# First layer's values and gate as seven block products instead of eight

## Chip, cores and metric

One core of a Trainium2 chip runs one program. The metric is the device time of one execution in microseconds, the median of three runs. Engine names in profile rows: PE is TensorE (PEld its weight loads), DVE is VectorE, ACT is ScalarE, POOL is GpSimd, SP is the queue that only issues transfers. Everything is computed in float32 by pairs: each operand of a matmul is split into a rounded part (`hi`) and a remainder (`lo`), and a product is the sum of three matmuls, hi by hi, hi by lo and lo by hi.

## The reference

The input is 512 tokens of width 1024, followed by a retention layer, a latent-attention layer and a third block with pooling, neighbourhood attention and an MLP. The change lies in the first layer, the part before its output projection:

```python
hproj = x @ w_in                       # 1024 -> 4*256 (q), 4*256 (k), 4*512 (v), 4*512 (gate)
q = rope(q); k = rope(k) * 256 ** -0.5
o[n] = sum over m <= n of gamma_h ** (n - m) * (q[n] . k[m]) * v[m]     # per head, 4 heads
o = (o - mean(o)) * rsqrt(var(o) + 1e-5)                                # per head and token, over 512
return (o * silu(gate)) @ w_out
```

## The kernel before

**Tiles.** `x` lies transposed in SBUF as `xhi` and `xlo`, eight tiles of 128 features by 512 tokens. The weights of one head come in six panels of 1 MB (128 by 2048): query, key, values (two panels of 512 features each), gate (two panels of 256 columns each). `split_dots` (L565 to L569) issues the three matmuls of a product; nearly all of them have 512 columns. PSUM has eight banks; A is the first four and B the last four.

**Panels.** For each panel SP loads it into one of two `stage` buffers (`load`, L576) once GpSimd is done with the panel before last. ScalarE rounds it to `whi` in two halves (`split_hi`, L1451), GpSimd subtracts to get `wlo`, also in two halves (`split_lo`, L718, L724). TensorE waits for each half.

**One head on TensorE** (`rest`, L984, and the loop at L1036): query and key, 48 matmuls each, into B; values for all four token tiles into A, 96; the scores, 24 narrower ones, into B; the first half of the gate, 48; the 30 matmuls of scores by values into B (L1002); the second half of the gate, 48; 16 transposes of the normed output (L1015). The gate is computed transposed, with its features on the partitions.

**VectorE** (loop at L2392) rotates query and key (L2399 to L2402 read PSUM, L2404 and L2405 read SBUF alone), makes the low parts of query, key, values and scores (`lo_of`, L2082), applies the decay, takes the statistics of the head's output (L2433 to L2443), norms it (L2447), and multiplies its transpose by the gate into `oT` (L2452). **ScalarE** (`head`, L1629) rounds what VectorE then subtracts from, and takes tanh and square root.

**Behind the heads** comes the output projection (`AO`), which is already computed as seven block products in 14 steps of 24 matmuls (`seven`, L953). It wants sums of weight blocks, made in DRAM while the heads run: ScalarE's queue issues copies (`copy_blocks`, L1506, four 1 MB copies at a time; `copy_b11`, `copy_b22` for a later stage) and GpSimd's queue issues transfers that add onto them (`sum_step`, L734; `up_sum`, L746). The steps of AO need an operand split (`operand_hi`, `operand_lo`, `combine`) and a panel split (`weights_hi`, `weights_lo`); VectorE makes most of those remainders, GpSimd those of the first two steps.

## Time and profile before

| | |
|---|---|
| median of 3 runs | 1414.61 us (1414.3 to 1414.74) |
| the profiled execution | 1414.12 us, of which the profile's span is 1412.3 us |
| TensorE | busy 1393.4 us, 99% of the span, granted clock 0.997 |
| VectorE, ScalarE, GpSimd | 65%, 49%, 27% of the span |
| DMA | 260 MB, mean 184 GB/s |
| heads 1 to 3 | 77.8 us each; head 0 ends at 84.5 us, head 3 at 319.65 us |

A busy share says how much of the time an engine had work. An engine's row in the timeline gives its start and its length; matmuls overlap, so what one costs is the distance between two starts, and not its length. The number in brackets behind a row is the time that the engine stood idle ahead of it, and what ended that.

### The profile page before, as it was taken

To read this page: it belongs to the slowest core of one execution; us is meant where nothing else is said; L and a number is where in the kernel's file an instruction comes from. 1 tells how busy PE (TensorE), PEld (TensorE's weight loads), DVE (VectorE), ACT (ScalarE), POOL (GpSimd) and SP (SyncE) were. 2 spreads that over 40 slices of the span, in tenths; PEclk is the share of its full clock that TensorE was granted. 3 is DMA by queue.
4 is the path that set the end of the run, shared out by engine and by line. 5 is a ranking of instruction groups with operands and counts; after the bars stand their busy time and mean duration, and the time that the engine had idled before them with its cause. 6 is when DMAs were issued, how large, how long until landed. Compare 5 with 4: busy or idle time off the path is not lost.

```text
span 1412.3 us, 19358 instructions
## 1 busy us (share of the span) xinstructions
PE 1393.4 (99%) x7412; PEld 1203.4 (85%) x7412; DVE 919.2 (65%) x1562; ACT 698.8 (49%) x1131; POOL 388.2 (27%) x192
## 2 busy tenths in 40 slices
PE   9999999999999999999999999999999899999998
PEld 7888888888889888888888888778888899998887
DVE  6444354549961865545544479946877878789896
ACT  4323232236554533443443356648956465666554
POOL 5334254541034343343334230035314100000000
PEclk9999999999999999999999999999999999999999
DMA  7257946946533988975796557353122576446552
GB/s 292 90 194 204 296 155 164 263 115 258 188 103 129 289 235 221 312 176 157 210 302 161 162 207 284 135 193 126 64 83 75 165 184 173 128 173 213 197 187 111
DMA packets 53890, 260.26 MB, mean 184 GB/s; under 512 B 5568, under 2 KB 10304, under 8 KB 28224
## 3 DMA queue, kind: packets, MB, share of 16 engines
q1 hardware_dynamic: 37152, 163.04, 33.3%
q0 software_dynamic: 5760, 41.95, 14.9%
q10 hardware_dynamic: 10912, 54.40, 11.3%
q8 instruction: 41, 0.67, 0.2%
q14 instruction: 25, 0.20, 0.0%
HBM read 252.03 MB, written 91.23 MB: 243 GB/s over the span
## 4 chain that ended last, share of the span: by engine, by line
PE 89%; DVE 7%; ACT 2%; POOL 1%; issue 1%; DMA 0%; SPq 0%; DVEq 0%; ACTq 0%; POOLq 0%
PE bank L567 23%; PE bank L569 23%; PE bank L568 23%; PE bank L1176 6%; PE bank L1238 4%; PE bank L1127 3%; PE bank L1155 1%; DVE wlo L2082 1%; DVE wlo_a L2082 1%; DVE xlo L2082 1%; DVE br_lo L2082 1%; PE bank L1318 0%; PE bank L913 0%; PE bank L1015 0%; DMA stage<-in_w 0%
## 5 line engine op out<-in xcount | busy, mean ns | idle before, releaser
L724 POOL TENSOR_TENSOR wlo<-stage,whi 128x1024 fp32r<-128x1024 f32 (+2 forms) x116 | 291.9, 2543 | 544.8 <-ACT whi L1458 544.8
L1458 ACT ACTIVATE whi<-stage 128x1024 fp32r<-128x1024 f32 (+2 forms) x120 | 122.2, 1069 | 87.3 <-PE bank L569 64.3
L567 PE MATMUL bank<-xhi,whi 128*128 128x512 f32 (+1 forms) x428 | 149.3, 349 | 3.2 <-DVE xlo L2082 1.8
L569 PE MATMUL bank<-xhi,wlo 128*128 128x512 f32 (+1 forms) x428 | 148.5, 347 | 0.0
L568 PE MATMUL bank<-xlo,whi 128*128 128x512 f32 (+1 forms) x428 | 148.3, 346 | 0.0
L1461 ACT ACTIVATE whi<-stage 128x1024 fp32r<-128x1024 f32 (+2 forms) x125 | 118.0, 989 | 40.3 <-PE bank L569 29.4
L2082 DVE TENSOR_TENSOR wlo<-stage,whi 128x1024 fp32r<-128x1024 f32 x108 | 123.4, 1168 | 14.7 <-ACT whi L1461 14.7
L567 PEld LDWEIGHTS bank<-xhi,whi 128*128 128x128 f32 x428 | 81.1, 189 | 13.5 <-issue 2.2
L567 PE MATMUL bank<-whi,xhi 128*128 128x512 f32 (+1 forms) x236 | 91.4, 387 | 1.1 <-POOL wlo L724 1.1
L569 PE MATMUL bank<-whi,xlo 128*128 128x512 f32 (+1 forms) x236 | 90.4, 383 | 0.0
L568 PE MATMUL bank<-wlo,xhi 128*128 128x512 f32 (+1 forms) x236 | 90.3, 383 | 0.0
L569 PEld LDWEIGHTS bank<-xhi,wlo 128*128 128x128 f32 x428 | 81.0, 189 | 10.3
L568 PEld LDWEIGHTS bank<-xlo,whi 128*128 128x128 f32 x428 | 81.1, 189 | 9.8
L2082 DVE TENSOR_TENSOR wlo_a<-stage,whi_a 128x1024 fp32r<-128x1024 f32 (+1 forms) x60 | 71.4, 1217 | 18.5 <-ACT whi_a L1461 18.5
L1461 ACT ACTIVATE whi_a<-stage 128x1024 fp32r<-128x1024 f32 (+1 forms) x56 | 53.8, 1008 | 22.8 <-PE bank L569 19.9
L567 PEld LDWEIGHTS bank<-whi,xhi 128*128 128x128 f32 x236 | 44.8, 190 | 10.4 <-POOL wlo L724 1.3
L569 PEld LDWEIGHTS bank<-whi,xlo 128*128 128x128 f32 x236 | 44.7, 190 | 8.4
L568 PEld LDWEIGHTS bank<-wlo,xhi 128*128 128x128 f32 x236 | 44.9, 190 | 8.0
L1176 PE MATMUL bank<-xhi,whi 128*128 128x512 f32 x128 | 50.7, 396 | 0.0
L1176 PE MATMUL bank<-xhi,wlo 128*128 128x512 f32 x128 | 50.0, 391 | 0.0
L1176 PE MATMUL bank<-xlo,whi 128*128 128x512 f32 x128 | 49.9, 390 | 0.0
L2082 DVE TENSOR_TENSOR pt_lo<-bank,pt_hi 128x384 fp32r<-128x384 f32 (+1 forms) x48 | 26.6, 595 | 34.9 <-ACT pt_hi L1461 34.9
(451 smaller groups left out, 3943.5 us busy)
## 6 DMA issues: line engine op xcount, KB each, us to landing
stage<-in_w SPq DMA_DIRECT2D x79, 1024.0 KB, 4.9
tsum<-in_w ACTq DMA_DIRECT2D x32, 1024.0 KB, 14.5
stage<-tsum SPq DMA_DIRECT2D x32, 1024.0 KB, 4.8
tsum<-in_w POOLq DMA_DIRECT2D x16, 1024.0 KB, 10.1
tsum<-tsum POOLq DMA_DIRECT2D x16, 1024.0 KB, 10.1
stage<-in_w SPq DMA_DIRECT2D x8, 1152.0 KB, 6.3
usum<-in_w POOLq DMA_DIRECT2D x8, 1024.0 KB, 9.9
stage<-usum SPq DMA_DIRECT2D x32, 256.0 KB, 3.8
```

Of the source, the lines that this page charges most:

```text
L567: pe.matmul(dst, a_hi, b_hi, start=start, stop=False)
L568: pe.matmul(dst, a_hi, b_lo, start=False, stop=False)
L569: return pe.matmul(dst, a_lo, b_hi, start=False, stop=stop)
L724: pool.tensor_tensor(lo[:, r], stage[p % 2][:, r], hi[:, r].bitcast(F32), ALU.subtract).then_inc(w_lo, 1)
L1127: last = pe.matmul(bank[4 + q][:, 0:w], left, right, start=i == 0, stop=i == 4)
L1155: last = pe.transpose(dst[min(kt, 2)][:, at:at + P], prob[:, src:src + P], ident[:, :])
L1176: last = pe.matmul(bank[0][:, :], left[:, k, f], right[:, k, :], start=i == 0, stop=i == 23)
L1238: last = pe.matmul(bank[m][:, :], left[:, k, m * P:(m + 1) * P], right[:, k, :], start=i == 0, stop=i == 23)
L1458: act.activation(parts(p)[0][:, r], stage[p % 2][:, r], ACT.Copy).then_inc(w_hi, 1)
L1461: act.activation(dst, src, ACT.Copy, scale=scale).then_inc(signal, 1)
L2082: dve.tensor_tensor(dst, src, hi.bitcast(F32), ALU.subtract).then_inc(signal, 1)
```

## The change

The values (512 columns) and the gate (512 columns) of a head are taken as one product of `x` with a weight block matrix of two by two: rows are the two halves of the 1024 features, columns are values (B11, B21) and gate (B12, B22). With the tokens in two halves too, that is eight block products of 256 tokens by 512 features by 512 columns, 24 matmuls each; the new form takes seven. It needs sums of `x` blocks (S1 to S4, once, in head 0), sums of weight blocks (T1 to T4, in every head), and sums of results.

- TensorE, per head: B11, key, B21 (onto B11's banks: values of the first token half), B22 by S4, scores, S1 by T1, S2 by T2, S3 by T3, A22 by T4, scores by values, next head's query, transposes. Banks go in pairs X, W, Y, Z.
- VectorE makes T1 to T4 (2048 wide) and their low parts, the S sums and theirs, twelve additions of results per head (`a_c`), low parts of values, gate multiplications from `th` and `gate` in SBUF, and a norm that takes the gate with it.
- ScalarE rounds nine panels per head, copies the first product aside (`kept1`), scales the normed tiles by the deviation, and moves the transposes to `oT`.
- GpSimd splits five panels per head; the order of its DMA sums changes; `up_sum(0, g)` comes behind the heads.
- SP loads six panels per head as before, in another order, into three buffers and free tiles. The load of `x` for the residual moves from the start to head 3.
- Copies are issued one by one behind T1, T2, T3 and T4 of heads 0 to 2; the eight of `copy_b22` one by one in steps 4 to 11 of AO.
- For head 3 the split of AO's first two operands lies ahead of T3; its transposes lie behind the first two steps of AO.

Core of the diff:

```diff
@@ TensorE
+            def head(h):
+                if h:
+                    pe.wait_ge(a_c, 12 * h)
+                block_product(h, A_B11, X)
+                turned_product(h, AK)
+                pe.wait_ge(a_k1, 2 * h + 2)
+                block_product(h, A_B21, X, True)
+                pe.wait_ge(a_q32, 4 * h + 3)
+                if h == 0:
+                    pe.wait_ge(vs_l, 1)
+                block_product(h, A_B22, Y)
                 pe.wait_ge(a_qklo, 4 * h + 4)
...
+                pe.wait_ge(a_vlo, 4 * h + 2)
+                if h == 0:
+                    pe.wait_ge(vs_l, 4)
+                block_product(h, A_T1, X)
+                pe.wait_ge(a_dec, 4 * h + 2)
+                block_product(h, A_T2, Z)
+                pe.wait_ge(a_dec, 4 * h + 4)
+                block_product(h, A_T3, W)
+                pe.wait_ge(a_c, 12 * h + 4)
+                block_product(h, A_T4, X)
...
+                inner(0, (0,))
+                inner(1, (0, 1))
+                inner(2, (0, 1))
+                inner(3, (0, 1))
+                pe.wait_ge(a_vlo, 4 * h + 3)
+                inner(2, (2,))
+                pe.wait_ge(a_vlo, 4 * h + 4)
+                inner(3, (2, 3))
...
+            for h in range(HA):
+                head(h)
+                if h + 1 < HA:
+                    pe.wait_ge(a_c, 12 * h + 10)
+                    turned_product(h + 1, AQ)
+                    turn_head(h)
             for d in range(13):
                 f, g = divmod(d, AO.dq)
+                if d == 2:
+                    turn_head(HA - 1)
@@ VectorE
+                rope(h, 0)
+                if h == 0:
+                    operand_sums()
+                rope_lo(h, 0)
+                if h == 0:
+                    for n in range(4):
+                        operand_sum_lo(n)
+                t1()
+                if h:
+                    t3()
+                rope(h, 1)
+                rope_lo(h, 1)
+                for q in range(2):
+                    v_low(q, X[q][:, :])
+                if h == 0:
+                    t3()
+                both(A_T1)
...
+                dve.tensor_tensor(s0, s2, s0, ALU.subtract).then_inc(g_sum, 1)
...
+                for i in range(TT):
+                    decays(h, i)
+                dve.wait_ge(g_sum, 3 + 4 * h + 3)
+                both(A_T2)
+                for i, kt in enumerate(S_ORDER):
...
+                    lo_of(s_lo[:, KT_AT[kt]:KT_AT[kt] + w], work[:, kt, 0:w], s_hi[:, KT_AT[kt]:KT_AT[kt] + w], a_slo)
...
+                dve.tensor_tensor(s0, a_staged(h, A_B21), s0, ALU.subtract).then_inc(g_sum, 1)
+                both(A_T3)
...
+                gates(0)
+                gates(1)
+                dve.wait_ge(a_m, 7 * h + 7)
...
+                for q in range(2, TT):
+                    dve.wait_ge(a_c, 12 * h + 9 + q)
+                    v_low(q, kept1[:, q - 2, :])
+                gates(2)
+                gates(3)
+                if h == HA - 1:
+                    combine(AO, 2)
@@ ScalarE
+                if h == HA - 1:
+                    act.wait_ge(a_ot, 4 * h)
+                    operand_hi(AO, 0)
+                    operand_hi(AO, 1)
+                head_hi(h, A_T3, (g_sum, 3 + 4 * h + 2), (a_m, 7 * h + 4))
...
+                    act.wait_ge(a_m, 7 * HA)
+                    weights_hi(AO, 1)
+                    operand_hi(AO, 2)
+                    weights_hi(AO, 2)
                 act.wait_ge(a_var, h + 1)
                 act.activation(small[:, 1, 0:TT], small[:, 0, 0:TT], ACT.Sqrt).then_inc(a_sd, 1)
...
+                for q in range(TT):
+                    act.wait_ge(a_on, 4 * h + q + 1)
+                    copy(onorm[:, q, :], onorm[:, q, :], a_sc, small[:, 2, q:q + 1])
@@ SP
+                sp.wait_ge(g_plo, 10 * h + 2)
+                head_load(h, A_B22)
+                if h:
+                    sp.wait_ge(a_on, 4 * h)
+                    head_load(h, A_B21)
+                sp.wait_ge(g_plo, 10 * h + 6)
+                head_load(h, A_B12)
@@ GpSimd
+            for h in range(HA):
+                for j in BY_POOL:
+                    if (h, j) == (0, AQ):
+                        continue
+                    head_lo(h, j)
...
             operand_lo(AO, 0)
             operand_lo(AO, 1)
+            weights_lo(AO, 0)
             weights_lo(AO, 1)
```

`rope(h, a)` is the six instructions of L2399 to L2405 (a is 0 for the query, 1 for the key); the third `a_q32` of a head is the key's L2404. `operand_sums` is four additions of 128 by 1024 in SBUF, `operand_sum_lo` one of 128 by 1024, `both(j)` two of 128 by 1024, `t1` and `t3` one of 128 by 2048 each. `t1` reads B12 and waits for its load. `BY_POOL` is query, B11, key, B21, B22, in that order.

## Rows read from the trace of the kernel before

**Rows 1.** Profile page: busy time and share of the span of each engine

```profile
PE 1393.4 (99%) x7412; PEld 1203.4 (85%) x7412; DVE 919.2 (65%) x1562; ACT 698.8 (49%) x1131; POOL 388.2 (27%) x192
```

**Rows 2.** Waits of TensorE to 520 us: total, times, longest

```profile
PE bank L1025 <- ACT xhi L1461: 1.6, 1, 1.6
PE bank L982 <- DVE qk_lo L2371: 1.5, 1, 1.5
```

**Rows 3.** Windows of head 1 and AO: us, busy PE, PEld, DVE, ACT, POOL, clock, DMA share, GB/s

```profile
84.50:162.30 77.80, 77.80 (x361) 64.97 (x359) 37.09 (x51) 23.69 (x31) 33.19 (x16) 1.00 0.84 247
...
319.65:397.00 77.35, 77.35 (x348) 64.07 (x348) 74.07 (x87) 47.80 (x55) 6.90 (x3) 1.00 0.56 208
```

**Rows 4.** Timeline of TensorE: start, length; first matmuls, then head 0

```profile
1.47 3.78 PE L982 MATMUL bank<-qk_lo 128*128 128x512 f32 x8 [1.47 <-DVE qk_lo L2371]
...
19.22 0.39 PE L567 MATMUL bank<-xhi,whi 128*128 128x512 f32 x1
...
30.10 0.39 PE L567 MATMUL bank<-whi,xhi 128*128 128x512 f32 x1
...
51.86 0.39 PE L567 MATMUL bank<-qk_hi 128*128 128x512 f32 x1
...
55.62 0.44 PE L567 MATMUL bank<-xhi,whi 128*128 128x512 f32 x1
```

**Rows 5.** Timeline of VectorE in head 1: the query's rotation and its low parts

```profile
99.04 0.68 DVE L2402 TENSOR_TENSOR work<-bank,rope_a 128x512 f32<-128x512 f32 x1
99.75 1.64 DVE L2404 TENSOR_TENSOR work<-work 128x512 f32<-128x512 f32 x1
101.31 2.88 DVE L2405 TENSOR_TENSOR work<-work 128x512 f32<-128x512 f32 x1
104.11 1.47 DVE L2082 TENSOR_TENSOR qk_lo<-work,qk_hi 128x512 fp32r<-128x512 f32 x2
```

**Rows 6.** Timeline of GpSimd in the same stretch, one instruction to a row

```profile
98.43 2.41 POOL L724 TENSOR_TENSOR wlo<-stage,whi 128x1024 fp32r<-128x1024 f32 x1 [7.50 <-ACT whi L1458]
...
100.79 2.85 POOL L724 TENSOR_TENSOR wlo<-stage,whi 128x1024 fp32r<-128x1024 f32 x1
```

**Rows 7.** Timeline of VectorE in head 0, the second of these instructions

```profile
22.55 0.69 DVE L2405 TENSOR_TENSOR work<-work 128x512 f32<-128x512 f32 x1
```

**Rows 8.** Groups by line and shape, 0 to 400 us: busy time, mean ns

```profile
L2082 DVE TENSOR_TENSOR wlo<-stage,whi 128x1024 fp32r<-128x1024 f32 x16 | 19.2, 1215 | 0.0
...
L2082 DVE TENSOR_TENSOR v_lo<-bank,v_hi 128x512 fp32r<-128x512 f32 x16 | 11.1, 692 | 47.9 <-ACT v_hi L1461 47.9
...
L765 POOL TENSOR_TENSOR ar_lo<-oT,ar_hi 128x1024 fp32r<-128x1024 f32 x2 | 4.8, 2406 | 3.0 <-ACT ar_hi L1461 3.0
```

**Rows 9.** Timeline of VectorE, end of head 3: statistics and norm

```profile
307.02 0.70 DVE L2433 BATCH_NORM_STATS2 stat<-bank 128x6 f32<-128x512 f32 x1 [2.02 <-PE bank L569]
...
308.61 0.18 DVE L2443 RECIPROCAL small<-small 128x4 f32<-128x4 f32 x1 [0.27 <-ACT small L1670]
308.82 2.96 DVE L2447 TENSOR_SCALAR work<-bank,mv,small 128x512 f32<-128x512 f32 x4
```

**Rows 10.** Timeline of ScalarE in the same stretch: panel rounding, table load

```profile
300.70 2.00 ACT L1461 ACTIVATE whi<-stage 128x1024 fp32r<-128x1024 f32 x2
302.71 1.28 ACT L1670 ACT_TABLE_LOAD   x1
```

**Rows 11.** DMA to 340 us: issues, KB each, median us to landing

```profile
stage<-in_w SPq DMA_DIRECT2D x25, 1024.0 KB, 5.0
tsum<-in_w ACTq DMA_DIRECT2D x8, 1024.0 KB, 10.4
```

**Rows 12.** Panel loads of line 580: issued 100 to 125 us, then 245 to 262

```profile
DMA to landing us min/median/max: 4.7/4.7/4.8
...
DMA to landing us min/median/max: 8.7/11.6/14.5
```

More of the change, by code:

```diff
@@ L585, in _ @@
             for c, r in enumerate(FIRST_W):
-                sp.dma_start(stage[0][:, r], t["w"][0, :, r]).then_inc(first[c] if c < 4 else landed[0], 16)
+                sp.dma_start(stage[0][:, r], t["w"][0, :, r]).then_inc(first[c] if c < 4 else a_ld[0], 16)
                 if c >= 3:
@@ new lines, in turned_product @@
+            def turned_product(h, j):
+                wh, wl = [w.rearrange("p (k n) -> p k n", k=KX) for w in a_parts(h, j)]
+                if h and j == AK:
+                    pe.wait_ge(a_ot, 4 * h - 2)
+                for m in range(2):
+                    c = slice(m * P, (m + 1) * P)
+                    for k in range(KX):
+                        if m == 0 and k in (0, KX // 2):
+                            head_need(h, j, k > 0)
+                        last = split_dots(pe, (W if j == AQ else Y)[m][:, :], wh[:, k, c], wl[:, k, c], xhi[:, k, :],
+                                          xlo[:, k, :], k == 0, k == KX - 1)
+                    last.then_inc(a_qk, 1)
@@ new lines, in block_product @@
+            def block_product(h, j, banks, onto=False):
+                wh, wl = [w.rearrange("p (k n) -> p k n", k=PK) for w in a_parts(h, j)]
+                x_hi, x_lo = a_operand(j)
+                for kk in range(PK):
+                    if kk % 2 == 0:
+                        head_need(h, j, kk > 0)
+                    for a in range(2):
+                        r = slice(a * P, (a + 1) * P)
+                        last = split_dots(pe, banks[a][:, :], x_hi[:, kk, r], x_lo[:, kk, r], wh[:, kk, :], wl[:, kk, :],
+                                          kk == 0 and not onto, kk == PK - 1, onto)
+                last.then_inc(a_m, 1)
@@ L1617, in _ @@
             for c, r in enumerate(FIRST_W):
-                act.wait_ge(first[c] if c < 4 else landed[0], 16)
+                act.wait_ge(first[c] if c < 4 else a_ld[0], 16)
                 copy(whi[0][:, r], stage[0][:, r], f_hi)
@@ L1623, in _, with head_hi @@
             act.wait_ge(f_hi, 5)
-            act.sem_inc(w_hi, 2)
-            split_hi(A0 + 1)
-            act.wait_ge(xt_lo, KX)
-            act.dma_start(xres[:, :, :], t["x"]).then_inc(aux["x"], 16)
+            act.sem_inc(g_hi, 2)
             A, B, E, O = bank[0:4], bank[4:8], bank[0::2], bank[1::2]
-            def head(h, last=False):
-                n = 6 * h
-                act.wait_ge(a_dec, 4 * h + 4)
+            X = bank[0:2]
+            def head_hi(h, j, ready, count):
+                act.wait_ge(*ready)
+                act.wait_ge(*count)
+                for b in range(2):
+                    r = slice(b * PAN // 2, (b + 1) * PAN // 2)
+                    copy(a_parts(h, j)[0][:, r], a_staged(h, j)[:, r], g_hi)
@@ L1655, in tanh @@
[L1655 to L1657 removed]
+                head_hi(h, A_B21, (a_ld[3], 16 * h + 16), (a_m, 7 * h + 1))
+                if h == 0:
+                    operand_sum_hi(3, 3)
+                for a in range(2):
+                    act.wait_ge(a_m, 7 * h + 1)
+                    copy(kept1[:, a, :], X[a][:, :], a_k1)
+                if h == 0:
+                    operand_sum_hi(0, 3)
+                    operand_sum_hi(1, 3)
+                    operand_sum_hi(2, 4)
@@ new lines, in head @@
+                head_hi(h, A_B22, (a_ld[0], 32 * h + 32), (a_qk, 4 * h + 4))
+                for m in range(2, 4):
+                    act.wait_ge(a_q32, 4 * h + (m + 1))
+                    copy(qk_hi[:, m, :], work[:, m % 2 * 2, :], a_qkhi)
+                for q in range(2):
+                    act.wait_ge(a_m, 7 * h + 2)
+                    copy(v_hi[:, q, :], X[q][:, :], a_vhi)
+                head_hi(h, A_T1, (g_sum, 3 + 4 * h + 1), (a_m, 7 * h + 2))
+                copy_step(h, 0)
```

474 lines of the change are left out of this document (293 added, 181 removed).

## The prediction, made before the changed kernel ran

> **What bounds the kernel now.** I read the page's busy times first: TensorE is busy 99% of the span [rows 1]. That alone doesn't say that it is the bound, so the waits of TensorE come next: to 520 us it waited for others 3.1 us, all of it ahead of the first products [rows 2]. The windows by stage say the same of head 1: 77.8 us long, TensorE busy 77.8, with VectorE, ScalarE and GpSimd between 24 and 37 us [rows 3]; heads 2 and 3 read alike. So a matmul taken out of the heads is worth its full distance to the next, as long as the other queues keep up. That distance is in the timeline: from 19.22 to 30.10 stand 48 matmuls and from 30.10 to 51.86 another 96, 0.2267 us each [rows 4].
>
> **The work removed.** Per head the values and the gate took 192 matmuls of 512 columns; seven products of 24 are 168. Query, key, scores, scores by values and transposes keep their number. 4 x 24 x 0.2267 = **21.8 us less**. Everything else in this sum is a wait of TensorE that the trace of before doesn't have, so the question is which queue comes late.
>
> **The price of an instruction on VectorE.** An instruction that reads PSUM takes 0.69 us for 512 columns, 0.60 from start to start [rows 5, 8]. One with both inputs in SBUF takes the same in head 0 [rows 7], but 1.64 and 2.88 us in head 1 [rows 5]. There GpSimd was in its own subtractions, 2.41 us alone: the first ended at 100.8, VectorE's L2404 ended 0.6 later, GpSimd's second took 2.85 in place of 2.41, and L2405 ended 0.6 behind that one [rows 5, 6]. I read from this that the two take turns, a whole instruction each. The Trainium skill ("SBUF — State Buffer", "Who interferes with whom") says the same as a rule: a VectorE instruction with two SBUF inputs and a GpSimd instruction that reads SBUF share a read port, and one blocks wholly for the other. By that rule the sum comes out as below, and without it at the first rival's 1392.8. It speaks against this change, which moves T sums, S sums, their remainders, gate products and half the values' remainders into SBUF. I take durations of 0.60, 1.14 and 2.2 us for 512, 1024 and 2048 columns (1.22 long for 1024 [rows 8]; 2048 is an estimate, twice that less the fixed part) and 2.38 for GpSimd's (two took 4.8 [rows 8]).
>
> **Head 0, the largest term.** TensorE's fourth item is B22, which waits for the key's L2404. TensorE comes to it at 19.1 + 5.4 (B11) + 10.9 (key) + 5.4 (B21) = 40.9 us. VectorE must do, from 19.3 on and ahead of that instruction: the query's rotation 3.7, four S sums 4.6, two low parts 1.2, four low parts of S 4.6, T1 2.2, the key's rotation 3.1; together 19.4, to 38.7. In that time GpSimd does key, B21 and B22, six instructions. I laid them out in turns: VectorE stands 1.4 ahead of the query's L2404, and 2.4 ahead of each of L2405, S4, S3 and the third and fourth low parts of S, 13.3 in all. That makes 52.1 us: **TensorE idle 11.2 us**. Below: nothing, if nothing blocks (38.7 is ahead of 40.9). Above: 12.5, with GpSimd at 2.6 us an instruction, between its 2.41 and 2.85 [rows 6]. I take 11.2, by the rows of head 1.
>
> **The clock behind it.** The eight matmuls at the start, which nothing ran ahead of, stand 0.47 us apart [rows 4], the pace of the lower level (1.2 GHz); from 19 us on it is 0.2267 at the upper (2.4). The trace has no idle stretch of 11 us later on, so what one does is not shown. Bounds: nothing, or the loss of the start, about 11 matmuls x 0.24 = 2.6 us. I take **2.0**, nearer to the start. The Trainium skill ("TensorE: Matmul & The Clock Gate", "What's actually happening") has it that idleness puts the array back to the lower level, which would be the upper bound here.
>
> **Heads 1 to 3, the other waits.** A head begins with B11 at 0. B12's load is issued when GpSimd has done the key, at 5.0, and lands 5.0 later [rows 11]; T1 can't begin ahead of 12.0, since GpSimd does B21 from 7.3 to 12.0. T1 and T3 end at 16.4, the key at 16.5, L2404 of its rotation at 20.7, and B22 is due at 21.8: no wait. The scores, T1, T2, T3 and T4 find their operands 1 to 3 us early. The values of the second half are the exception. Their low parts stand behind two gate products, each behind one of GpSimd's two halves of the next query; they end 5.1 us behind T4, and the 21 matmuls ahead cover 4.8. **0.3 a head in heads 0 to 2**, 0.9. ScalarE, busy for 24 of 78 us before [rows 3], and GpSimd, with ten instructions a head in place of twelve, wait on others and cost nothing of their own.
>
> **Head 3** has AO's first operands in it. Two GpSimd remainders of 2.4 fall between VectorE's score remainders and T4, a chain that was 2.0 early: 4.8 - 2.0 = **2.7** ahead of T3. AO's first panel stands where the next query stood and gives **1.1** ahead of the values.
>
> **The last transposes** come behind two steps of AO, 10.9 us. The chain from the last of the scores by values: the fourth gate product, behind GpSimd, 2.0; GpSimd again 2.4; `combine` 1.1; then ScalarE rounds operand 2 and panel 2, 3.0 [rows 10], loads its table 1.3 [rows 10], takes the root; reciprocal and four norms 3.2 [rows 9]; the last scaled copy 0.7. About 13.9, so **3.0** waited. Before, the same cover of 10.9 hid a chain of 5 us.
>
> **AO itself.** VectorE is the fuller queue there, 74 of 77 us [rows 3], and in the new order it begins each step 1 to 2 us ahead of TensorE, where it was about 3. I count nothing for it. Transfers are as many as before, but `up_sum`, `copy_b22` and the load of `x` fall into it; a panel may land 11 us after its issue before TensorE waits, against 5.0 [rows 11]. Nothing, with the bound in the rivals.
>
> **Sum:** -21.8 + 11.2 + 2.0 + 0.9 + 2.7 + 1.1 + 3.0 = -0.9. The profiled execution took 1414.1 (span 1412.3 and 1.8 around it) and the median of the runs is 0.5 above it; from the median, **1413.7 us**.
>
> **Rivals.** *The waits cost less.* If VectorE and GpSimd hardly delayed each other, none of the waits above would be left, and the kernel would take 1414.6 - 21.8 = 1392.8; with half of the waits left (9.5) and a clock that falls for half as long, 1403 to 1404. For it: some SBUF instructions slip into a gap, as in head 0 [rows 7], and head 0's order depends on starts that I know to a microsecond or two. Against: rows 5 and 6 show the turns in every head. *B12 lands late*, the one on the other side. Its place is T1 in heads 1 to 3. Up to 7 us from issue to landing nothing happens; from there each microsecond goes to B22's wait, with a GpSimd turn on top: 1.5 us a head at 8, 2.5 at 9, 5 at 11.6. It decides from about 7.8 us on (3 x 1.2 is slower by 0.2%); at 11.6, three times 5 less 0.7 of head 3's wait give 1428. For it: panel loads behind a burst of copies landed at 8.7 to 14.5 us [rows 12], and the sum onto DRAM that GpSimd issues ends, at 10 us from its issue, only 2 us ahead of this load. Against: alone they take 4.7 [rows 12], and the copies now come singly, the last of a head 30 us ahead of this load. *AO's panels land late*: 13 us gives 4.5 more, 15 gives 12, so 1418 to 1426. Against: three steps of 5.4 us lie between issue and use. That the seven products aren't seven isn't a rival: they can be counted.
>
> **Chances.** Forecast 0.45, its own range 1410 to 1418 (the clock's bounds, and 2 us either way on head 3's waits). Waits cost less 0.30. B12 late 0.17, AO late 0.08. About 0.2% (2.8 us) is what a measurement of this kernel can tell from no change. Faster: all of the second and 0.08 of the first, 0.38. Slower: 0.20 of the late loads and 0.02, 0.22. The rest, 0.40, is the same. The range leaves out the full gain (0.12) and the worst of the late loads (0.08): 1401 to 1423.
>
> **What would show it.** In the changed profile: 24 matmuls fewer a head; a wait of TensorE on the key's L2404 at 41 us, about 11 us long, then matmuls 0.4 apart or more for some microseconds; VectorE's S sums and their low parts at 2.4 to 3.5 us each where GpSimd runs; heads 1 and 2 about 72.5 us long; waits of 3 us ahead of T3 of head 3 and ahead of the last transposes. Wrong: no wait in head 0, or key rotations of 0.69 us; waits on B22 in heads 1 to 3; panels of AO late.

## The result, and the profile after

The changed kernel takes **1419.84 us**, median of 13 runs (1415.76 to 1422.22), beside 1414.14 for the kernel before (13 runs, 1411.76 to 1416.94). The ratio is 1.0040, 95% interval 1.0031 to 1.0049: slower by 0.4%, 5.7 us, where 0.9 us less was forecast. The profiled execution took 1421.21, span 1419.2, which is 6.9 us above the span of before. Page of the changed kernel, busy times, to be read beside [rows 1]:

```profile
PE 1379.0 (97%) x7316; PEld 1189.6 (84%) x7316; DVE 1048.7 (74%) x1650; ACT 745.0 (52%) x1197; POOL 373.6 (26%) x184
```

96 matmuls fewer, as counted; VectorE has 130 us more to do. The waits of TensorE to 430 us (total, times, longest), which answer to [rows 2], say where the gain went:

```profile
PE bank L613 <- DVE work L2602: 10.5, 1, 10.5
PE bank L1000 <- DVE xres L2457: 5.7, 2, 4.1
PE bank L1167 <- ACT onorm L1614: 2.3, 1, 2.3
PE bank L613 <- DVE wlo L2283: 2.1, 1, 2.1
...
PE bank L613 <- DVE v_lo L2283: 0.5, 1, 0.5
```

In order of time, TensorE waited 10.5 us for the key's rotation in head 0 (L2602 is the old L2404), 2.1 ahead of T3 in head 3, 0.5 for the values of its second half, 2.3 ahead of the last transposes (L1167), and 5.7 ahead of the first two transposes behind AO (L1000), which wait for the normed tiles (L2457). The windows (us, busy PE, PEld, DVE, ACT, POOL, clock, DMA share, GB/s) of the wait in head 0, of head 1, and of the stretch from AO's first matmul to the second of those transposes, then the same stretch of the kernel before, where head 3's 16 transposes stand ahead of AO:

```profile
41.00:57.00 16.00, 5.85 (x15) 4.60 (x16) 15.87 (x15) 4.10 (x6) 3.69 (x2) 0.57 0.21 66
...
102.81:175.34 72.53, 72.53 (x336) 60.40 (x335) 63.53 (x71) 34.70 (x47) 28.35 (x14) 1.00 0.65 199
...
312.43:401.78 89.35, 81.34 (x361) 66.79 (x359) 82.50 (x97) 51.93 (x63) 10.76 (x8) 0.98 0.80 260
```

```profile
317.74:396.61 78.87, 78.87 (x361) 65.59 (x360) 74.77 (x87) 49.51 (x57) 6.60 (x3) 1.00 0.56 203
```

Head 1 is 72.5 us long and full, beside 77.8 in [rows 3]: 5.3 us a head, near the 5.44 of 24 matmuls. The first and the last window are where it is lost again. Two marks show how much. In the kernel before, TensorE stood ahead of AO and its 16 transposes at 317.74 and began the second transposes behind AO at 396.61; in the changed one, at 312.43 and 401.78. So it comes to AO **5.3 us earlier** (21.8 less 16.5 lost in the heads) and leaves it **5.2 later**: AO, with the last transposes, costs 10.5 us more. 1.7 more are lost behind that, 1.4 of them at once: from the start of the second transposes to the fourth matmul behind them the kernel before took 1.6 us (396.61 to 398.18) and the changed one 3.0 (401.78 to 404.79), behind its wait of 4.1 and with a granted clock of 0.84 between 396 and 407 us.

What fails in AO is seen on VectorE. First the kernel before: VectorE's first remainder in AO and its second norm, then TensorE's first and second transposes (start, length):

```profile
325.42 1.22 DVE L2082 TENSOR_TENSOR s_lo<-comb,s_hi 128x1024 fp32r<-128x1024 f32 x1 [2.36 <-POOL wlo L758]
...
394.50 1.28 DVE L2256 SCALAR_TENSOR_TENSOR xres<-oT,small,rows 128x1024 f32<-128x1024 f32 x1
```

```profile
392.97 1.04 PE L913 MATMUL bank<-ident,xres 128*128 128x128 f32 x8
396.61 1.03 PE L913 MATMUL bank<-ident,xres 128*128 128x128 f32 x8
```

Then the same of the changed kernel, with every stop of VectorE on the way that is longer than 0.4 us, GpSimd's only split in that stretch, and TensorE's second transposes:

```profile
324.79 1.22 DVE L2283 TENSOR_TENSOR s_lo<-comb,s_hi 128x1024 fp32r<-128x1024 f32 x1
...
330.65 1.23 DVE L2283 TENSOR_TENSOR ar_lo<-comb,ar_hi 128x1024 fp32r<-128x1024 f32 x1 [1.23 <-ACT ar_hi L1614]
...
352.65 2.36 DVE L2283 TENSOR_TENSOR wlo<-stage,whi 128x1024 fp32r<-128x1024 f32 x2 [0.97 <-ACT whi L1614]
...
364.30 1.23 DVE L2283 TENSOR_TENSOR wlo<-stage,whi 128x1024 fp32r<-128x1024 f32 x1 [2.36 <-ACT whi L1614]
...
398.33 3.39 DVE L2457 SCALAR_TENSOR_TENSOR xres<-oT,small,rows 128x1024 f32<-128x1024 f32 x1
```

```profile
398.30 5.65 POOL L792 TENSOR_TENSOR wlo<-stage,whi 128x1024 fp32r<-128x1024 f32 x2 [47.20 <-DVE wlo_a L2283]
```

```profile
401.78 1.54 PE L1000 MATMUL bank<-ident,xres 128*128 128x128 f32 x6 [4.10 <-DVE xres L2457]
```

Before, VectorE's chain of instructions took 325.42 to 395.78, 70.4 us with one stop of 0.3, and TensorE came 0.8 us behind its end: AO had **next to no room on VectorE**. In the changed kernel that chain begins only 0.6 earlier, since the norm of head 3 stands ahead of it, and it grows by 6.6: 1.2 for operand 3 (ScalarE was still copying transposes), 1.0 and 2.4 for panels, and 2.1 at the second norm, where GpSimd's split took the turn 0.03 us ahead. 324.8 + 70.4 + 6.6 is 401.8, where TensorE goes on. The panels were late, as e2 below shows, because of the transfers that the change put into AO. DMA issues from 335 to 400 us (KB each, median us to landing), where the same loads took 4.7 and 4.8 before:

```profile
stage<-in_w SPq DMA_DIRECT2D x7, 1024.0 KB, 9.3
stage<-tsum SPq DMA_DIRECT2D x4, 1024.0 KB, 8.8
usum<-in_w ACTq DMA_DIRECT2D x7, 512.0 KB, 14.0
usum<-in_w POOLq DMA_DIRECT2D x2, 1024.0 KB, 12.7
```

### The profile page after: what moved, and what is told of

The parts are those of the page before. It is cut to its first block, busy times and chain, and to the rows that moved or that the text cites. A ratio compares the mean times of both kernels' runs of the same rounds, so it can differ in the third digit from the quotient of the medians.

```text
span 1419.2 us, 19150 instructions
## 1 busy us (share of the span) xinstructions
PE 1379.0 (97%) x7316; PEld 1189.6 (84%) x7316; DVE 1048.7 (74%) x1650; ACT 745.0 (52%) x1197; POOL 373.6 (26%) x184
## 4 chain that ended last, share of the span: by engine, by line
PE 77%; DVE 16%; ACT 3%; DMA 1%; issue 1%; POOL 1%; ACTq 0%; DVEq 0%; POOLq 0%
PE bank L613 20%; PE bank L615 20%; PE bank L614 20%; PE bank L1329 6%; PE bank L1391 4%; PE bank L1280 3%; DVE wlo L2283 3%; PE bank L1308 1%; DVE wlo_a L2283 1%; DMA stage<-in_w 1%; DVE s_lo L2283 1%; PE bank L1167 1%; DVE gate L2651 1%; DVE br_lo L2283 1%; DVE xres L2336 1%
## 5 line engine op out<-in xcount | busy, mean ns | idle before, releaser
L792 POOL TENSOR_TENSOR wlo<-stage,whi 128x1024 fp32r<-128x1024 f32 (+2 forms) x70 | 175.9, 2538 | 380.1 <-ACT whi L1611 332.7
L613 PE MATMUL bank<-xhi,whi 128*128 128x256 f32 (+1 forms) x300 | 98.9, 330 | 3.2 <-DVE xlo L2283 1.8
L615 PE MATMUL bank<-xhi,wlo 128*128 128x256 f32 (+1 forms) x300 | 98.6, 329 | 0.0
L614 PE MATMUL bank<-xlo,whi 128*128 128x256 f32 (+1 forms) x300 | 98.6, 329 | 0.0
L841 POOL TENSOR_TENSOR wlo<-stage,whi 128x1024 fp32r<-128x1024 f32 x22 | 58.5, 2678 | 94.6 <-ACT whi L1614 94.6
L613 PEld LDWEIGHTS bank<-xhi,whi 128*128 128x128 f32 x300 | 57.1, 190 | 8.7 <-issue 2.2
L615 PEld LDWEIGHTS bank<-xhi,wlo 128*128 128x128 f32 x300 | 57.1, 190 | 5.0
L614 PEld LDWEIGHTS bank<-xlo,whi 128*128 128x128 f32 x300 | 57.1, 190 | 5.0
L1614 ACT ACTIVATE whi<-oT 128x1024 fp32r<-128x1024 f32 x34 | 34.1, 1053 | 36.5 <-DVE oT L2689 17.3
L613 PE MATMUL bank<-ql_hi,whi 128*128 128x512 f32 x120 | 46.9, 391 | 0.0
```

Of the source, the lines that this page charges most:

```text
L613: pe.matmul(dst, a_hi, b_hi, start=start, stop=False, skip_group_check=onto)
L614: pe.matmul(dst, a_hi, b_lo, start=False, stop=False, skip_group_check=onto)
L615: return pe.matmul(dst, a_lo, b_hi, start=False, stop=stop, skip_group_check=onto)
L792: pool.tensor_tensor(lo[:, r], stage[p % 2][:, r], hi[:, r].bitcast(F32), ALU.subtract).then_inc(w_lo, 1)
L841: pool.tensor_tensor(lo[:, r], a_staged(h, j)[:, r], hi[:, r].bitcast(F32), ALU.subtract).then_inc(g_plo, 1)
L1614: act.activation(dst, src, ACT.Copy, scale=scale).then_inc(signal, 1)
```

## Experiments

Medians of all runs; the ratio is to the kernel before, on the same chip. e1 to e15 ran on four chips, on which the kernel before took 1413.5 to 1414.1, so a difference of two medians can be off by 0.6 us for that alone. A trace shows one execution, which can lie over 4 us from the median. "Quiet" stands for e2's edit (copies and sums out of AO), "tail" for the four of e7.

| run | median us | ratio, 95% interval |
|---|---|---|
| changed kernel | 1419.84 | 1.0040 (1.0031 to 1.0049) |
| e1 key first | 1415.59 | 1.0016 (1.0007 to 1.0025) |
| e2 quiet AO | 1416.24 | 1.0009 (0.9997 to 1.0021) |
| e3 fill | 1418.79 | 1.0038 (1.0025 to 1.0052) |
| e4 GpSimd in pieces | 1418.72 | 1.0033 (1.0023 to 1.0044) |
| e5 key first, quiet | 1412.23 | 0.9981 (0.9968 to 0.9993) |
| e6 key first, B21 on VectorE | 1414.35 | 1.0007 (0.9998 to 1.0016) |
| e7 quiet, tail | 1407.07 | 0.9953 (0.9939 to 0.9966) |
| e8 e6, quiet, tail | 1405.84 | 0.9940 (0.9927 to 0.9954) |
| e9 e8, head 0 again | 1405.97 | 0.9941 (0.9925 to 0.9957) |
| e10 e9, AO's panels on VectorE | 1404.35 | 0.9927 (0.9911 to 0.9944) |
| e11 copies alone out of AO | 1418.14 | 1.0031 (1.0017 to 1.0045) |
| e12 quiet, tail, fill | 1408.86 | 0.9960 (0.9945 to 0.9975) |
| e13 quiet, norm alone | 1413.66 | 1.0000 (0.9991 to 1.0009) |
| e14 quiet, T3 alone | 1413.51 | 0.9996 (0.9987 to 1.0006) |
| e15 quiet, table alone | 1414.55 | 1.0007 (0.9998 to 1.0016) |

### e1: the key first in head 0

```diff
                 if h == 0:
-                    for n in range(4):
-                        operand_sum_lo(n)
-                t1()
-                if h:
+                    operand_sum_lo(0)
+                else:
+                    t1()
                     t3()
                 rope(h, 1)
                 rope_lo(h, 1)
+                if h == 0:
+                    for n in range(1, 4):
+                        operand_sum_lo(n)
+                    t1()
...
-                if h == 0:
-                    t3()
                 both(A_T1)
+                if h == 0:
+                    t3()
```

> Head 0 on VectorE: the key's rotation and its low parts go ahead of three of the four low parts of S and of T1 (T3 goes behind T1's low parts). Theory 'order': TensorE's 10.5 us on the key's L2602 is what stands ahead of it; with 7.4 us of work (3.4 + 1.2 + 2.3, and the turn) moved behind, that wait falls to 2 to 4 us. Part comes back ahead of T1's product, whose low parts are then VectorE's last, 2 to 4 us. Together 4 to 8 us less in 1419.8, so 1412 to 1416, and less of it at the lower clock level. Rival 'the work itself': VectorE has too much to do in head 0 up to T1, whatever the order; what leaves the first wait comes back ahead of T1 whole, and the time stays within 2 us of 1419.8.

Measured: 4.3 us less by the medians. The wait for the key is 0.3; waits of 2.7, 1.3 and 0.4 stand ahead of T1, T2 and T3 instead. All that is left of the low clock in head 0's records is one stretch of 3.4 us, where the changed kernel had 13.7. "Order" holds in part: over half of the wait was order; the rest comes back ahead of T1 to T3.

### e4: GpSimd's splits in pieces

```diff
-                    pool.tensor_tensor(lo[:, r], a_staged(h, j)[:, r], hi[:, r].bitcast(F32), ALU.subtract
-                                       ).then_inc(g_plo, 1)
+                    for e in range(2):
+                        r = slice((2 * b + e) * PAN // 4, (2 * b + e + 1) * PAN // 4)
+                        last = pool.tensor_tensor(lo[:, r], a_staged(h, j)[:, r], hi[:, r].bitcast(F32), ALU.subtract)
+                    last.then_inc(g_plo, 1)
```

> GpSimd splits the heads' panels in pieces of 512 columns in place of 1024 (twice as many instructions, signalled as before). Theory 'turns of a whole instruction': VectorE stands for one piece, 1.2 us in place of 2.4, so its instructions with both inputs in SBUF take 1.8 to 2.2 us where they took 2.9 to 3.4; in head 0, where six of them stood ahead of the key, the key's L2602 ends 5 to 8 us earlier, TensorE's wait falls from 10.5 to 3 to 5 us; the values' and gate's chain in head 3 gains 2 to 4 us. 1411 to 1416. Rival 'the port is held as long as GpSimd has work': VectorE's instructions take 2.9 to 3.4 as before, nothing changes. Rival 'pieces cost GpSimd too much': its splits get longer by over 1 us a panel and TensorE waits on wlo.

No difference that can be told, and the wait is 9.3 for 10.5. VectorE's sums and low parts of S in the changed kernel, and in this run:

```profile
26.54 1.21 DVE L2623 TENSOR_TENSOR gate<-xres 128x1024 f32<-128x1024 f32 x1
27.78 1.23 DVE L2625 TENSOR_TENSOR onorm<-gate,xres 128x1024 f32<-128x1024 f32 x1
29.04 3.30 DVE L2627 TENSOR_TENSOR onorm<-xres,onorm 128x1024 f32<-128x1024 f32 x1
32.27 3.43 DVE L2628 TENSOR_TENSOR gate<-xres 128x1024 f32<-128x1024 f32 x1
...
39.10 3.40 DVE L2283 TENSOR_TENSOR vs_a<-onorm,vs_a 128x1024 fp32r<-128x1024 f32 x1
42.42 3.36 DVE L2283 TENSOR_TENSOR vs_b<-gate,vs_b 128x1024 fp32r<-128x1024 f32 x1
```

```profile
24.36 2.31 DVE L2625 TENSOR_TENSOR gate<-xres 128x1024 f32<-128x1024 f32 x1
26.71 2.18 DVE L2627 TENSOR_TENSOR onorm<-gate,xres 128x1024 f32<-128x1024 f32 x1
28.92 2.20 DVE L2629 TENSOR_TENSOR onorm<-xres,onorm 128x1024 f32<-128x1024 f32 x1
31.04 2.32 DVE L2630 TENSOR_TENSOR gate<-xres 128x1024 f32<-128x1024 f32 x1
...
40.06 2.31 DVE L2285 TENSOR_TENSOR vs_a<-onorm,vs_a 128x1024 fp32r<-128x1024 f32 x1
42.30 2.28 DVE L2285 TENSOR_TENSOR vs_b<-gate,vs_b 128x1024 fp32r<-128x1024 f32 x1
```

The turn is one instruction of GpSimd, as expected: 2.2 us stood in the first, 1.1 in the second. But there are twice as many, and now nearly every instruction stands. From the first L2602 to the key's rotation VectorE took 27.0 us (20.92 to 47.90) in the changed kernel and 26.2 here (21.53 to 47.77), for 13.8 us of work at the prediction's durations. None of the three theories had that: between these two traces cutting the turns moved the standing about, and its sum stayed.

### e6: B21 of head 0 on VectorE

```diff
+                    if (h, j) == (0, A_B21):
+                        pool.wait_ge(g_plo, 8)
+                        continue
                     head_lo(h, j)
...
                 dve.tensor_tensor(s2, s1, a11, ALU.subtract).then_inc(vs_s, 1)
+                dve.wait_ge(g_plo, 6)
+                head_lo(0, A_B21, 0, g_plo)
+                head_lo(0, A_B21, 1, g_plo)
```

> The run with the key ahead, and in head 0 VectorE makes B21's low parts (two instructions of 1024 columns, 1.14 us each) in place of GpSimd (two of 2.4 and more). Theory 'one port, the work adds up': each us that GpSimd reads SBUF is one that VectorE's SBUF work stands, however it is cut; taking 4.8 us off GpSimd gives VectorE 4.2 us of standing back for 2.3 of work, so its chain to T1 is about 1.9 shorter, and the waits of 2.7 and 1.6 ahead of T1's product and the next shrink by that: 1413.7 (1412.5 to 1414.5). Rival 'GpSimd's work is free outside a turn': VectorE gets 2.3 more to do, the waits grow to 6, and it takes 1417 to 1418.

1414.35, 1.2 below e1, inside the first theory's interval and 2.7 or more below the rival's. The two intervals of the ratios overlap, so the size isn't sure; the sign of the rival is out. VectorE got more work and its chain got no longer, since it does the work in half of GpSimd's time.

### e9: head 0 once more

T1 goes ahead of the low parts of S, the last of those behind T1's low parts, and T3 behind T2's low parts; TensorE waits for the last of S only ahead of T3's product. The rest is e8.

> The run with all edits, and in head 0 what TensorE doesn't need yet goes further back on VectorE: T1 ahead of the low parts of S, the last low part of S behind T1's low parts, T3 behind T2's low parts. Theory 'VectorE is late in head 0 alone, and has room behind it': the waits of 2.5 ahead of T1 and 2.7 ahead of T2 shrink to 1 or less each, and the low clock behind the second goes: 4 to 6 us less than 1405.8, 1400 to 1402. Rival 'VectorE is full up to T3': the waits turn up ahead of T3 or T4 in the same size, 1404 to 1406.

1405.97 beside 1405.84: the rival. e8 had two waits in head 0, 4.9 us together; this run has three, ahead of T1, T2 and T3 (start, length of the first matmul; in brackets the wait):

```profile
52.36 0.47 PE L613 MATMUL bank<-whi,vs_a 128*128 128x512 f32 x1 [1.34 <-DVE wlo L2296]
...
59.56 0.47 PE L613 MATMUL bank<-whi,vs_a 128*128 128x512 f32 x1 [1.49 <-DVE wlo L2296]
...
67.85 0.47 PE L613 MATMUL bank<-whi,vs_b 128*128 128x512 f32 x1 [2.56 <-DVE wlo L2296]
```

5.4 us together. VectorE is full in head 0 up to T3; with e1 and e6 some 5 us of wait stay in both orders that were tried.

### e2 and e11: AO without copies and sums

```diff
+                if h == 3:
+                    copy_b22(2 * k)
+                    copy_b22(2 * k + 1)
...
-                if 4 <= d < 12:
-                    copy_b22(d - 4)
...
+            pool.wait_ge(t_sum, 16 * 8)
+            up_sum(0, 0)
             operand_lo(AO, 0)
             operand_lo(AO, 1)
+            up_sum(0, 1)
             weights_lo(AO, 0)
+            up_sum(0, 2)
             weights_lo(AO, 1)
-            pool.wait_ge(t_sum, 16 * 8)
-            for g in range(4):
-                up_sum(0, g)
+            up_sum(0, 3)
```

> The eight copies onto the second sum (0.5 MB each) go from steps 4 to 11 of AO to head 3, two behind each of T1 to T4, and GpSimd's four sums onto DRAM go from behind AO's panels to between the splits of head 3, so that AO has its panel loads nearly alone. Theory 'late panels': AO's end is set by VectorE, which stood 1.0 and 2.4 us for panels that landed 9 to 13 us after their issue; these waits go, loads take 5 us as before, TensorE's wait of 5.7 us on the first norm falls to about 2, the low clock behind it too: 3.5 to 6 us less, 1414 to 1416. Rival 'VectorE is full in AO anyway': the panels that came late only used up slack, and under 1 us comes back. Rival 'moved, not removed': head 3's loads land late instead, and TensorE waits ahead of T1 to T4 there.

3.6 us less. Panels land in 4.7 and 4.8 us again, VectorE's two waits for panels, 3.3 us, are gone, and TensorE's on the norm is 2.7. From AO's first matmul to the second transposes its trace takes 85.9 us, 3.4 less than the changed kernel's 89.4. The waits of TensorE on the norm, in e2 and then in e7 (below):

```profile
PE bank L1002 <- DVE xres L2458: 2.7, 1, 2.7
```

```profile
PE bank L1003 <- DVE xres L2465: 1.3, 1, 1.3
```

e11 has the first half of the diff alone:

> The changed kernel with the eight copies moved from AO to head 3, and GpSimd's four sums left where they are, in AO's window. It tells which of the two made the panels late (both moved gave 3.6 us). Theory 'the copies': 8 of the 12 transfers, and the only ones between 350 and 387 us: 3 to 4 us less than 1419.8, about 1416.5, and VectorE waits under 0.5 us for panels. Rival 'the sums': each takes 10 to 13 us and the last two run while the late panels are loaded: under 1 us comes back, 1419 or more, with panels still 9 us or more from issue to landing at 340 to 360 us.

1418.14, 1.7 less, between the two; its interval overlaps that of the changed kernel. In its trace one wait of VectorE for a panel is left, 1.5 of the 3.3 us. So the copies are part of it and the sums are too; how it divides isn't settled, since the trace is of its fastest execution (1414.71). That trace also lacks the wait of 2.1 ahead of T3, which e2, with the same copies in head 3, still has.

### e7 and its parts: the way from T3 of head 3 to the norm

On top of e2's edit:

```diff
+                head_hi(h, A_T3, (g_sum, 3 + 4 * h + 2), (a_m, 7 * h + 4))
                 if h == HA - 1:
                     act.wait_ge(a_ot, 4 * h)
                     operand_hi(AO, 0)
                     operand_hi(AO, 1)
-                head_hi(h, A_T3, (g_sum, 3 + 4 * h + 2), (a_m, 7 * h + 4))
...
                     weights_hi(AO, 1)
+                    act.activation(eps[:, 2:3], eps[:, 0:1], ACT.Sqrt)
                     operand_hi(AO, 2)
...
-                    turned_out(HA - 1)
-                rounded(AO, d)
+                    turned_out(HA - 1, (0, 1, 2))
+                    operand_hi(AO, d)
+                    turned_out(HA - 1, (3,))
+                    weights_hi(AO, d)
+                    keep(AO, d)
+                else:
+                    rounded(AO, d)
...
             pool.wait_ge(w_lo, 2 * (B0 + 1))
+            pool.wait_ge(n_x, 2)
```

> The run with the quiet AO, and four edits on the way from T3 of head 3 to the first norm: AO's first two operands are rounded behind T3's rounding and not ahead of it; ScalarE's square root table is loaded ahead of operand 2, while ScalarE waits for VectorE; operand 3 is rounded ahead of the last of the four copies behind the transposes; GpSimd's split of the next stage's panel waits for the second normed tile. Theory 'VectorE's chain sets AO's end, each wait in it counts': the wait of 2.1 ahead of T3 goes, that ahead of the last transposes falls from 2.3 to 1, the norm's L2457 takes 1.28 in place of 3.4 and the wait on it 0 to 0.5 in place of 2.7. 2.1 + 1.3 + 2.5 = 5.9 below the quiet run's 1416.2, 1410.3 (1409 to 1412). Rival 'TensorE is the bound again there': only the two waits ahead of AO come off, 3.4, and the norm's edits give nothing, 1412.8.

1407.07, 9.2 below e2, more than either theory. In the trace the wait ahead of T3 is gone, that of the last transposes is 1.4, the second norm takes 1.28 and TensorE waits 1.3 for it; the stretches at the lower clock behind those two waits are gone as well. VectorE's chain in AO is 70.5 us long, as before. Neither theory counted the clock behind the norm. Between the two traces, which both have the wait of 10.5 in head 0, e7 gains 2.3 us up to AO, 3.9 from AO's first matmul to the second transposes (82.0 for 85.9), and 1.9 behind them, 8.1 together. Taken apart:

> The quiet kernel (1416.2) and one of the tail's edits alone: GpSimd's split of the next stage's panel waits for the second normed tile. Theory 'port at the norm, and the clock behind it': the second L2457 takes 1.28 in place of 3.4, TensorE's wait there falls from 2.7 to 0.6 (2.1 less), and without that wait the 3.4 us stretch at the lower clock behind it goes, 1.7 more: 1412.4 (1411.5 to 1413.5). Rival 'the clock gives nothing back': 2.1 alone, 1414.1. Rival 'GpSimd's split is then what comes late': TensorE waits on wlo for the same time, 1416.

> The quiet kernel and the second of the tail's edits alone: AO's first two operands are rounded behind T3's rounding in head 3, so that GpSimd's remainders of them no longer fall between the scores' remainders and T3's. Theory: VectorE's sum for T4 takes 2.28 in place of 4.49, T3's low parts come in time, TensorE's wait of 2.1 there goes and everything behind is that much earlier: 1414.1 (1413.3 to 1415). Rival 'head 3's end is set by GpSimd's later turns anyway': the wait goes, but the last transposes wait 2 us longer and AO's VectorE chain begins no earlier: 1416.

> The quiet kernel and the last two of the tail's edits: the square root's table is loaded while ScalarE waits for operand 2, and operand 3 is rounded ahead of the last of four copies. Theory 'waits and the clock behind them': the wait ahead of the last transposes falls from 2.3 to 1.0 and the 3.4 us at the lower clock behind it go (1.3 + 1.7), and VectorE's AO chain begins 1.3 earlier and loses 0.9 less: TensorE's wait at the norm, 2.7, falls a little. 1413 (1412 to 1414). Rival 'no clock in it': 1.3 to 2.2 less, 1414 to 1415. With the two runs beside it the gains add to 9.2 if the clock counts, to 6 if it doesn't.

By the medians 2.6, 2.7 and 1.7 less than e2, each of them with its own wait gone or nearly gone from the trace; in e15's TensorE gained 2.1 at the transposes and waited 0.7 longer at the norm. But e2's runs lie 8.4 us apart, and the intervals of all three ratios overlap that of e2. By the ratios the three gain 1.3, 1.8 and 0.3 us, 3.4 in sum, beside 7.9 for the four edits together; by the medians it is 7.0 beside 9.2. So no theory of the three is settled, nor what the clock gives back behind these waits; only the four edits together stand clear of e2. In the traces AO's stretch, 85.9 us in e2, is 83.4, 84.9 and 82.9.

### e3 and e12: the low clock filled

```diff
+                if h == 0:
+                    for i in range(40):
+                        pe.matmul(bank[7][:, :], xhi[:, 0, 0:P], xhi[:, 0, :], start=True, stop=True)
                 pe.wait_ge(a_q32, 4 * h + 3)
```

> 40 matmuls of 512 columns, whose results are thrown away, stand ahead of TensorE's wait for the key in head 0: 40 x 0.2267 = 9.1 us of work in a wait of 10.5. Theory 'idle time lowers the clock': the matmuls behind the wait stand 0.227 apart from the first on, the 13.7 us stretch at 0.5 in the clock's records goes, and the time falls by 2.5 to 3 us, to about 1417. Rival 'the slow matmuls have another cause' (their operand has just been written, or the engine that writes it shares something with TensorE): 0.43 us apart as before, no change, or up to 1 us more.

> The 40 filling matmuls again, now in the kernel with quiet AO and mended tail (1407.1), in which the stretch behind head 0's wait is the only one at the lower clock up to the end of AO. Theory 'idle time lowers the clock': the stretch of 10 to 14 us at 0.5 goes, 2 to 3 us less, 1404.1 to 1405.1. Rival 'it is given back, as in the first fill': 1406.5 to 1407.5.

On the spot the first theory holds: in both traces the stretch behind the wait is gone from the records of the granted clock. The first matmuls behind the wait in e3 stand 0.23 apart from the second on:

```profile
52.00 0.50 PE L613 MATMUL bank<-whi,vs_b 128*128 128x512 f32 x1 [0.79 <-DVE work L2605]
52.34 0.39 PE L614 MATMUL bank<-wlo,vs_b 128*128 128x512 f32 x1
52.57 0.39 PE L615 MATMUL bank<-whi,vs_b 128*128 128x512 f32 x1
```

The traces have the gain, too: from B22's first matmul in head 0 to AO's first matmul the changed kernel took 261.3 us and e3 258.9; e7 took 258.8 and e12 256.5. That is 2.4 us less with the filling in both pairs. In the medians nothing is seen, 1.1 less in one and 1.8 more in the other, both within the intervals. Two things in the traces bear on that. Behind AO's second transposes e3's trace takes 2.1 us longer than the changed kernel's, with a granted clock of 0.69 between 396 and 407 us for 0.84. And in e13's execution the wait in head 0 was 6.3 and not 10.5 (below); there 9.1 us of filling would cost more than they give. How often either happens wasn't counted, so the cause stays open.

### e5, e8, e10: edits together

> Both edits of the first two runs together: the key ahead in head 0, and the copies and sums out of AO. Theory 'in series': what TensorE waits in head 0 moves everything behind it, AO's VectorE chain too, and the late panels lengthen that chain by themselves, so the two gains add: 4.3 and 3.6 below 1419.8, 1412 (1410.5 to 1413.5), below the kernel before. Rival 'the second covers the first': if AO waits for something that head 0 doesn't move (a transfer, or GpSimd's queue), the sum of the gains isn't reached, and it stays at 1414 to 1416.

1412.23: the gains add, and the kernel is faster than before by 0.2%.

> All edits that shorten a chain, together: key ahead, B21 on VectorE in head 0, quiet AO, and the four edits of the tail. In series the gains add: 4.3 + 1.9 + 3.6 + 5.9 = 15.7 below 1419.8, 1404.1 (1402 to 1407), 0.7% below the kernel before; TensorE keeps some 2.5 us of wait in head 0, 1 ahead of the last transposes. If the waits only move (VectorE is full over the heads as a whole), it stays above 1410.

1405.84, inside the range, but not by the sum: the tail gave 9.2 by the medians where 5.9 was added, and the two edits of head 0 give only 1.2 on top of e7, where 6.2 was added. That it came out is luck in part. In the traces they bring AO's first matmul from 310.82 to 305.26, 5.6 us earlier; but e7's trace is of its slowest execution, 4.2 above its median, and has the long wait in head 0.

> The kernel of the run before in this list, and VectorE splits AO's first two panels (four instructions of 1.14) in place of GpSimd (four of 2.4 to 2.7). Theory 'one port, the work adds up': the gate products of head 3 take 0.6 us apiece in place of 1.7 to 3.2; of the 8 us that they and the next stood, the chain to the last norm gets 2.5 to 3 net, so the last transposes wait 0 to 0.5 in place of 1.7 and AO's VectorE chain begins 2.5 to 3 earlier: 2 to 3 us below the run before it. Rival: VectorE, with 4.6 us more work, is later at the last norm: TensorE's wait there grows to 3 or more, and the time is 1 to 3 above the run before it.

The edit takes GpSimd's `weights_lo` of panels 0 and 1 out and puts the same two pairs of instructions on VectorE, behind the second gate product and behind `combine`. Head 3's four gate products in e9, then here:

```profile
296.07 5.15 DVE L2667 SCALAR_TENSOR_TENSOR gate<-th,gate 128x512 f32<-128x512 f32 x2
...
303.80 6.59 DVE L2667 SCALAR_TENSOR_TENSOR gate<-th,gate 128x512 f32<-128x512 f32 x2
```

```profile
295.39 1.28 DVE L2665 SCALAR_TENSOR_TENSOR gate<-th,gate 128x512 f32<-128x512 f32 x2
...
301.52 1.29 DVE L2665 SCALAR_TENSOR_TENSOR gate<-th,gate 128x512 f32<-128x512 f32 x2
```

VectorE's chain in AO begins at 312.94, in e9 at 317.53; the last transposes don't wait, and the second transposes behind AO begin at 383.78 in place of 388.02. 1404.35 is 1.6 below e9, a little less than was expected, and the two intervals overlap; behind those transposes e10's trace takes 1.9 us longer than e9's, which nothing here explains. By its median it is the fastest version: **0.9927 of the kernel before, 0.7% faster (0.9911 to 0.9944)**. Of the 21.8 us its trace has 12.8 at the second transposes (383.78 for 396.61). What is missing up to there is some 5 in head 0, for VectorE's work, and waits of under 1 us each; 2.6 more are lost behind.

## Why the prediction was wrong

Step by step, against the profiled execution:

- **The work removed, 21.8.** Right: 96 matmuls, 5.3 us a head in heads 1 and 2 (5.4 was forecast).
- **Head 0, 11.2.** Right: 10.5, by the mechanism that was given. The instructions that were laid out as standing are those that stood (L2602 2.89, L2603 2.89, and the four of 3.3 to 3.4 shown above); VectorE stood 13.2 us in all (27.0 less 13.8 of work), where 13.3 were laid out. The rule of the Trainium skill ("SBUF — State Buffer", "Who interferes with whom") agrees with these rows. How near it came is luck in part: of the traces without an edit in head 0 the changed kernel's, e2, e7, e11 and e14 have a wait of 10.1 to 10.5, e13 and e15 one of 6.3. That it isn't the length of a turn that sets the wait was not seen, and e4 showed it.
- **The clock, 2.0.** Right in kind and near in size at head 0; the first matmuls behind the wait, start and length:

```profile
51.15 0.79 PE L613 MATMUL bank<-whi,vs_b 128*128 128x512 f32 x1 [10.50 <-DVE work L2602]
51.74 0.63 PE L614 MATMUL bank<-wlo,vs_b 128*128 128x512 f32 x1
52.17 0.63 PE L615 MATMUL bank<-whi,vs_b 128*128 128x512 f32 x1
52.59 0.63 PE L613 MATMUL bank<-whi,vs_b 128*128 128x512 f32 x1
```

  They stand 0.43 apart, the lower level (1.2 GHz), 12 of them before it is 0.23 again: 12 x 0.2 = 2.4 us, and the window from 41 to 57 us above has a granted clock of 0.57. The Trainium skill ("TensorE: Matmul & The Clock Gate", "What's actually happening"), by which idleness puts the array back to the lower level, agrees with that. The fills put the price at 2.4 (above). But it was counted once; the records of the granted clock have the lower level twice more, 3.4 us each, behind the waits for the last transposes and the norm.
- **The other waits of the heads.** 0.9 in heads 0 to 2: none came. T3 in head 3: 2.1 for 2.7. The values in head 3: 0.5 for 1.1. With head 0 and the clock, 16.5 lost up to AO where 17.9 were forecast: this half was 1.4 us too dear. (Two of the sums are 0.1 off: the standing in head 0 adds up to 13.4, and 4.8 - 2.0 is 2.8.)
- **The last transposes, 3.0.** 2.3.
- **AO itself, counted at nothing. This step failed.** It cost 10.5 us with the last transposes, 8.2 without their wait, and 1.7 behind. The sentence "it begins each step 1 to 2 us ahead of TensorE ... I count nothing for it" saw that VectorE was the fuller queue, 74 of 77 us [rows 3], and then priced what is late there by whether TensorE waits for a panel. The profile of before had the right number: VectorE's second norm ended 0.8 us ahead of TensorE. With TensorE 5.3 us earlier and VectorE 0.6, AO was VectorE's to end, and each of its stops counted whole. e2 took out the stops for panels, e7 nearly all: in e7's trace the chain is 70.5 us again, and from AO's first matmul to the second transposes it takes 82.0 us, where the changed kernel took 89.4 and the kernel before 78.9. The medians fall by 12.8 together, with the wait ahead of T3, which isn't in AO, among what went.
- **The rivals.** "AO's panels land late" (0.08) was the nearest. Its place was wrong: it decided from 11 us to landing, by TensorE's wait; at a median of 9 they cost VectorE 3.3. "B12 lands late" did not come. "The waits cost less" did not come, though single executions can go that way (below).

The sum in the prediction's terms: -21.8 + 16.5 to AO + 10.5 in it + 1.7 behind = +6.9, the difference of the two spans. The 1.7 behind AO is the least sure of them: in the traces of e1 to e15 that stretch takes 1016.4 to 1019.5 us, in the changed kernel's 1017.4 and before 1015.7.

## What to carry to other kernels

When work is taken off the busiest engine, ask of every stage which engine is second and by how much, at the point where the stage is handed on; a queue that is 96% busy in one stage, as VectorE was in AO, can take the gain of all stages ahead of it, and a late transfer there is then paid for even if the busiest engine never waits for that transfer. Where VectorE's instructions with two SBUF inputs met GpSimd's splits, the two came near to one queue (e4: 14 us of VectorE's work took 26 to 27 us beside GpSimd's six splits of 2.4, whole or in halves): add up the times that fall together, and in a stretch where VectorE is short, try giving it GpSimd's splits, which took it half the time (1.14 us for 2.4; e6, e10). Shortening single waits pays in full only while the engine behind them isn't the late one. And read a trace as one execution: the same code had two courses here.

## What was not expected of the hardware

**Cutting GpSimd's instructions in half gave nothing** (e4): 1.1 us stood per turn in place of 2.2, in twice as many turns.

**Head 0 has two courses.** e13, whose code up to head 3 is that of e2, waited 6.3 us in head 0, where e2 waited 10.4. In e13 VectorE's L2604 (the changed kernel's L2602) came 0.08 us ahead of GpSimd's second panel; VectorE, then GpSimd:

```profile
20.66 0.69 DVE L2604 TENSOR_TENSOR work<-work 128x512 f32<-128x512 f32 x1
21.27 2.90 DVE L2605 TENSOR_TENSOR work<-work 128x512 f32<-128x512 f32 x1
24.09 3.43 DVE L2625 TENSOR_TENSOR gate<-xres 128x1024 f32<-128x1024 f32 x1
```

```profile
18.38 2.42 POOL L841 TENSOR_TENSOR wlo<-oT,whi 128x1024 fp32r<-128x1024 f32 x1
20.74 5.70 POOL L841 TENSOR_TENSOR wlo<-stage,whi 128x1024 fp32r<-128x1024 f32 x2
26.40 6.71 POOL L841 TENSOR_TENSOR wlo<-oT,whi 128x1024 fp32r<-128x1024 f32 x2
```

It took 0.69 where it took 2.89 in the changed kernel's trace, ScalarE got the query 2.4 us earlier, and GpSimd's third panel followed its second without a gap, so that VectorE's low parts of S fell into a stretch without GpSimd. From L2604 to the key's rotation VectorE took 22.5 us (20.66 to 43.20) for the work that took 27.0 in the changed kernel. So less than 0.1 us at the start goes with 4 us in that head, by these two traces; e15's trace has the same course. The spread of the changed kernel's runs, 6.5 us, is of that size; whether it comes from there wasn't tried.

**The same at the norm**: GpSimd's split began 0.03 us ahead of VectorE's L2457 and cost 2.1. In e5 the same instruction took 1.28, without an edit there.
